# Order of VectorE and ScalarE where a transformer trunk changes over to block products on Trainium2

## The chip, the cores and the metric

The kernel runs on one core of a Trainium2 chip. The metric is the device time of one execution in microseconds; a version's time is the median of its runs. A core has TensorE (matrix products, at a clock that the chip grants it), VectorE, ScalarE, GpSimd (POOL in the profile) and SyncE (SP, which issues most transfers from memory). The engines run side by side and wait for each other on semaphores only; each takes its own instructions in their order.

## The reference, cut to what matters

The reference is a trunk of two layers over 512 tokens of width 1024 in float32. Each layer mixes tokens (two kinds of attention and a convolution, gated) and then applies a feed-forward part with 2816 hidden columns:

```python
for l in range(DEPTH):                      # 2 layers
    ...                                     # token mixing, x = x + y @ w_out[l]
    h = rmsnorm(x, norm_ffn_g[l])
    ff = jax.nn.silu(h @ w_ffn_gate[l]) * (h @ w_ffn_up[l])
    x = x + ff @ w_ffn_down[l]
```

Only the two products `h @ w_ffn_gate` and `h @ w_ffn_up` matter here.

## The kernel before, in words

**Precision.** Each float32 product is made of three passes with operands rounded for TensorE: high x high, low x high, high x low. So every weight chunk in a `raw` buffer needs a cast by ScalarE (`w_hi`, signalled on `hi_done`) and a subtraction by VectorE (`w_lo` = raw - high, signalled on `lo_done`). Four `raw` buffers form a ring that SP refills. The same is done for the activations: `h_hi` and `h_lo`.

**Two ways of making the gate and up columns.** The first six of 22 column tiles (`FRONT`) are made plainly: twelve tiles (gate, up, gate, up, ..., c = 0 to 11), 24 matmuls of 512 columns each (line 1869), each evacuated by VectorE in `front_tile` (product with `rstd_x`, L1277), with ScalarE's SiLU behind every gate tile (L1100). The other 16 are made in eight turns (`fast_turn`) of seven block products, in the manner of Strassen and Winograd: gate and up weights, and the four quadrants of the normalised activations `h_norm`, are added and subtracted in quarters so that seven products replace eight. A block product is 24 matmuls of 256 columns (L2184) and adds one to `mm_done`.

**What the first turn needs.** The four weight quarters of a turn lie in the ring: `RAW_G2`, `RAW_G1`, `RAW_U1`, `RAW_U2` (slots 0 to 3). VectorE makes the sums `first_a` = G1 + G2 and `first_b` = `first_a` + U1 (`weight_sum`, L1652, signalled on `sum_done`). ScalarE casts quarters with `cast_raw` (L1073) and sums with `cast_sum` (L1079); VectorE makes their low parts with `low` (L1649). Product 1 multiplies U1 (slot 0) by the activation quadrant `b11`; product 2 multiplies `first_a` (slot 4) by `t0`; product 3 `first_b` (slot 2) by `t1`; product 4 U2 by `b21`; product 5 takes a later sum in slot 1, product 6 one in slot 2 with `b22`, product 7 takes G2. `t0` to `t3` are differences of quadrants, made ahead. The quadrants' high parts (`half_cast`, L1067) overwrite `h_hi`, which tile 11 still reads: `b11` may be cast when tile 11's first four k steps are through (`h_free`), `b21` and `b22` when tile 11 is done. Their low parts are `half_low` (L1656).

**Order.** All orders are written out by hand. On VectorE: tile 9's work, the sum `first_a`, a wait for two casts, the sum `first_b`, the eviction of tile 10, the low parts of `first_a` and of U1, the low half of `b11`, the low part of `first_b`, the low half of `b21`, and then the turn. On ScalarE: cast of `first_a`, cast of U1, SiLU of tile 10, cast of `first_b`, `b11`, `b21`, `b22`, then G2. `LO_U1 = 1, LO_S1 = 2, LO_S2 = 3, LO_G2 = 4, LO_U2 = 5, LO_S3 = 6, LO_S4 = 7` are the places of a turn's low parts on `lo_done`; in the first turn product 1 waits for the first two. SP refills G2's slot on the fourth low part, G1's on the turn's third sum and U1's and U2's on the sixth low part. Product 7 waits for VectorE's eviction into `q5_t` (L1768), which stands behind the low part of the next turn's U1.

Of the kernel before, what the change touches and what calls it, by code (L numbers as in the profile page):

```python
# [73 lines left out]
FRONT = 6  # L74
# [78 lines left out]
RAW_G2, RAW_G1, RAW_U1, RAW_U2 = 0, 1, 2, 3  # L153
LO_G2, LO_U2, LO_S3, LO_S4, LO_U1, LO_S1, LO_S2 = 4, 5, 6, 7, 1, 2, 3
# [85 lines left out]
def trunk(nc, dram, out):  # L240
# [121 lines left out]
    first_a = at("first_a", r0 + 80 * KB, [P, 1024])  # L362
    first_b = at("first_b", r0 + 84 * KB, [P, 1024])
# [15 lines left out]
    with ExitStack() as ctx:  # L379
# [9 lines left out]
        hi_done = sem("hi_done")  # L389
        lo_done = sem("lo_done")  # L390
# [53 lines left out]
        sum_done = sem("sum_done")  # L444
# [35 lines left out]
        as_k = lambda t: t[:].rearrange("p (k c) -> p k c", k=4)  # L480
# [268 lines left out]
        def _(act):  # L749
# [168 lines left out]
            for l in layers([(ev, EVENTS), (evac, EVACS), (sqa, SQUARES), (stat, 6), (own, 1), (lr, 5), (mt, EVENTS), (olo, HEADS), (vt, PAIRS),  # L918
# [150 lines left out]
                def cast_raw(slot, which, prev):  # L1069

                    act.wait_ge(raw_ready[which], rr[which].add(16))
                    act.wait_ge(mm_done, prev)
                    nc.scalar.copy(w_hi[slot][:], raw[which][:]).then_inc(hi_done, 1)  # L1073

                def cast_sum(slot, of, n, prev):

                    act.wait_ge(sum_done, sums.value + n)
                    act.wait_ge(mm_done, prev)
                    nc.scalar.copy(as_k(w_hi[slot]), of).then_inc(hi_done, 1)  # L1079
# [9 lines left out]
                for c in range(2 * FRONT):  # L1089
                    if c < 2 * FRONT - 2:  # L1090
                        split(FF + c + 2)
                    elif c == 2 * FRONT - 2:
                        ev.add()
                        cast_raw(0, RAW_U1, ev.value)
                    if c == 0:
                        root(x_std, D, 0)
                    evac.add()
                    if c % 2 == 0:
                        act.wait_ge(evac_done, evac.value)
                        nc.scalar.activation(tmp[2][:], tmp[0][:], ACT.Silu).then_inc(sig_done, 1)  # L1100
                    for k in T_LOWS.get(c, ()):
                        act.wait_ge(half_raw, 4 * l + k + 1)
                        half_cast(t_hi[k][:], t_raw[k][:])
                    if c == 2 * FRONT - 3:
                        cast_sum(4, as_k(first_a), 1, ev.value)
                cast_sum(2, as_k(first_b), 2, ev.value)
                act.wait_ge(h_free, l + 1)
                ev.add()
                for name in HALF_ORDER:
                    if name == "b21":  # L1110
                        act.wait_ge(mm_done, ev.value)
                    if name[0] == "b":
                        r, c = int(name[1]) - 1, int(name[2]) - 1
                        half_cast(quad(h_hi, r, c), quad(h_norm, r, c))
                    elif name in LATE:
                        k = int(name[1])
                        half_cast(t_hi[k][:], t_raw[k][:])
# [95 lines left out]
        def _(dve):  # L1213
# [244 lines left out]
            for l in layers([(hi, SPLITS - 2), (mm, EVENTS), (out_n, EVACS), (own, OWN), (taps, CT * TAPS), (sig, 4 + 24 + FRONT),  # L1458
# [188 lines left out]
                def low(slot, of):  # L1647
                    dve.wait_ge(hi_done, hi.add())
                    nc.vector.tensor_tensor(as_k(w_lo[slot]), of, as_k(w_hi[slot]).bitcast(F32), ALU.subtract).then_inc(lo_done, 1)  # L1649

                def weight_sum(to, a, b):
                    nc.vector.tensor_tensor(to, a, b, ALU.add).then_inc(sum_done, 1)  # L1652
# [30 lines left out]
                for c in range(2 * FRONT - 1):  # L1683
                    if c == 0:
                        split(FF + 2)
                        factor(x_std, rstd_x)
                    front_tile(c)
                    if c == 2 * FRONT - 2:
                        dve.wait_ge(sum_done, sums.value + 2)
                        low(4, as_k(first_a))  # L1690
                        low(0, raw_k[RAW_U1])
                    elif c:
                        split(FF + c + 2)
                    if c in (H_NORM_AT, H_NORM_AT + 1):
                        for k in range(4 * (c - H_NORM_AT), 4 * (c - H_NORM_AT) + 4):
                            ins = normal(k)
                        if c > H_NORM_AT:
                            mine(ins)
                    if c == T_SUMS_AT:
                        nc.vector.tensor_tensor(t_raw[0][:], quad(h_norm, 0, 0), quad(h_norm, 0, 1), ALU.subtract).then_inc(half_raw, 1)  # L1700
                        dve.wait_ge(half_raw, 4 * l + 1)
                        nc.vector.scalar_tensor_tensor(t_raw[1][:], t_raw[0][:], -1.0, quad(h_norm, 1, 1), ALU.mult, ALU.subtract).then_inc(half_raw, 1)
                    if c == T_SUMS_AT + 1:
                        nc.vector.tensor_tensor(t_raw[2][:], quad(h_norm, 1, 1), quad(h_norm, 0, 1), ALU.subtract).then_inc(half_raw, 1)
                        dve.wait_ge(half_raw, 4 * l + 2)
                        nc.vector.scalar_tensor_tensor(t_raw[3][:], t_raw[1][:], -1.0, quad(h_norm, 1, 0), ALU.mult, ALU.subtract).then_inc(half_raw, 1)
                    for k in T_LOWS.get(c, ()):
                        half_low(t_lo[k][:], t_raw[k][:], t_hi[k][:])
                    if c == 2 * FRONT - 3:
                        first_sum(as_k(first_a))  # L1710
                        dve.wait_ge(hi_done, hi.value + 2)
                        dve.wait_ge(sum_done, sums.value + 1)
                        weight_sum(as_k(first_b), as_k(first_a), raw_k[RAW_U1])

                def half_of(name):
                    if name[0] == "t":
                        k = int(name[1])
                        half_low(t_lo[k][:], t_raw[k][:], t_hi[k][:])
                    else:
                        r, c = int(name[1]) - 1, int(name[2]) - 1  # L1720
                        half_low(quad(h_lo, r, c), quad(h_norm, r, c), quad(h_hi, r, c))

                half_of("b11")
                low(2, as_k(first_b))
                half_of("b21")

# [125 lines left out]
        def _(pe):  # L1852
# [234 lines left out]
            for l in layers([(lo, SPLITS), (part, 5 * FAST), (half, 3 * FAST), (ev, EVACS), (ea, UP_COPIES), (fl, FEEDS), (sqa, SQUARES), (std, 5), (ex, STEPS),  # L2087
# [101 lines left out]
                def fast_turn(x, start=False):  # L2189

                    y_b, q_b = bank[6], bank[7]
                    pe.wait_ge(lo_done, lo.value + (LO_S1 if start else LO_U1))
                    halves_made = HALVES_MADE * l
                    pe.wait_ge(half_lo, halves_made + HALF_AT["b11"])
                    pe.wait_ge(part_out, part.value - 5)
                    product(x, W_SLOT[0], quad(h_hi, 0, 0), quad(h_lo, 0, 0), True, False)
                    pe.wait_ge(lo_done, lo.value + LO_S1)
                    pe.wait_ge(half_out, half.value)
                    product(q_b, 4 if start else W_SLOT[1], t_hi[0], t_lo[0], True, False)
                    pe.wait_ge(lo_done, lo.value + LO_S2)  # L2200
                    pe.wait_ge(part_out, part.value + 1)
                    product(x, W_SLOT[2], t_hi[1], t_lo[1], False, False)
                    pe.wait_ge(lo_done, lo.value + LO_U2)
                    pe.wait_ge(half_lo, halves_made + HALF_AT["b21"])
                    pe.wait_ge(half_out, half.value - 2)
                    product(y_b, W_SLOT[3], quad(h_hi, 1, 0), quad(h_lo, 1, 0), True, True)
                    pe.wait_ge(lo_done, lo.value + LO_S3)
                    pe.wait_ge(half_lo, halves_made + HALF_AT["t2"])
                    pe.wait_ge(part_out, part.value + 3)
                    product(x, W_SLOT[4], t_hi[2], t_lo[2], False, False)  # L2210
                    pe.wait_ge(lo_done, lo.value + LO_S4)
                    pe.wait_ge(half_lo, halves_made + HALF_AT["b22"])
                    pe.wait_ge(part_out, part.value + 2)
                    product(q_b, W_SLOT[5], quad(h_hi, 1, 1), quad(h_lo, 1, 1), False, True)
                    pe.wait_ge(lo_done, lo.value + LO_G2)
                    pe.wait_ge(half_lo, halves_made + HALF_AT["t3"])
                    pe.wait_ge(half_out, half.value + 2)
                    product(x, W_SLOT[6], t_hi[3], t_lo[3], False, True)
                    lo.add(PRODUCTS)
                    part.add(5)  # L2220
                    half.add(3)
# [112 lines left out]
```

## Time and profile before

| | |
|---|---|
| median of 3 runs | 1709.31 us (1708.85 to 1709.51) |
| the profiled execution | 1708.57 us |
| its span | 1706.8 us |
| TensorE busy | 1686.7 us |
| VectorE busy | 1202.2 us |
| ScalarE busy | 768.3 us |
| GpSimd busy | 194.5 us |

The span is what the profile covers of one execution; 1.8 us of that execution lie around it. Ends of matmuls are modelled, so TensorE's busy share is not the share of its peak; its granted clock averages 0.997 of full speed. The change to the block products comes once in each layer, near 566 us and near 1406 us.

### The profile page before, as it was taken

Reading aid. Unit: us, or ns where it says so; the run is one execution under the profiler, and the core shown is the slowest. Engines: PE = TensorE matmul, PEld = TensorE weight load, DVE = VectorE, ACT = ScalarE, POOL = GpSimd, SP = SyncE. Lnnn points to the kernel's source line nnn. Section 1 sums busy time; section 2 is a strip of 40 time slices with the busy share of each in tenths; the row PEclk is TensorE's granted clock in tenths of the full one; section 3 lists DMA queues with packets and bytes.
Section 4 is the critical chain, followed back from the end, with each engine's and each line's share of the span. In section 5 each row is a group of like instructions: output and inputs, shape, how many; then the busy total and the mean of one; then the engine's idle time right before and its main releaser. Section 6 shows DMA issues by size and latency. Waiting matters only on the chain.

```text
span 1706.8 us, 24438 instructions
## 1 busy us (share of the span) xinstructions
PE 1686.7 (99%) x9060; PEld 1404.0 (82%) x9060; DVE 1202.2 (70%) x1699; ACT 768.3 (45%) x1236; POOL 194.5 (11%) x125
## 2 busy tenths in 40 slices
PE   9999999999999999999999999999999999999998
PEld 7777777878788899988878777778788879999887
DVE  6898887966547787763359998877755577888422
ACT  4655444343343544552245554452533434556322
POOL 0830000010020000000126210000101100000010
PEclk9999999999999999999999999999999999999999
DMA  6341221333333233333333322214333323334332
GB/s 167 81 108 50 62 55 33 110 95 95 108 99 88 74 111 103 112 97 100 93 94 71 93 62 52 55 44 111 93 92 112 98 86 100 100 98 118 90 90 74
DMA packets 277166, 152.53 MB, mean 89 GB/s; under 512 B 30356, under 2 KB 276366, under 8 KB 277068
## 3 DMA queue, kind: packets, MB, share of 16 engines
q1 hardware_dynamic: 276760, 150.96, 31.7%
q8 instruction: 63, 1.03, 0.2%
q10 hardware_dynamic: 308, 0.25, 0.1%
q14 instruction: 35, 0.29, 0.1%
HBM read 149.09 MB, written 2.10 MB: 89 GB/s over the span
## 4 chain that ended last, share of the span: by engine, by line
PE 90%; DVE 5%; ACT 2%; issue 1%; DMA 1%; POOL 1%; SPq 0%; ACTq 0%; DVEq 0%; POOLq 0%
PE bank L1869 50%; PE bank L2184 17%; PE bank L1983 12%; PE bank L2016 2%; PE bank L1995 2%; PE bank L1938 2%; PE bank L1954 1%; PE bank L2269 1%; DVE w_lo L1239 1%; DMA raw<-in_w_ffn_up 1%; PE bank L1923 1%; POOL ln_acc L640 1%; DMA raw<-in_w_in 1%; PE bank L1910 1%; ACT w_hi L1073 0%
## 5 line engine op out<-in xcount | busy, mean ns | idle before, releaser
L764 ACT CAST w_hi<-raw 128x1024 fp32r<-128x1024 f32 (+3 forms) x243 | 223.7, 921 | 464.6 <-PE bank L1869 458.0
L1239 DVE TENSOR_TENSOR w_lo<-raw,w_hi 128x1024 fp32r<-128x1024 f32 (+3 forms) x243 | 264.6, 1089 | 155.7 <-ACT w_hi L764 154.6
L1869 PE MATMUL bank<-h_hi,w_hi 128*128 128x512 f32 x672 | 267.1, 397 | 0.7 <-DVE w_lo L1239 0.4
L1869 PE MATMUL bank<-h_hi,w_lo 128*128 128x512 f32 x672 | 262.0, 390 | 0.0
L1869 PE MATMUL bank<-h_lo,w_hi 128*128 128x512 f32 x672 | 261.8, 390 | 0.0
L1316 DVE SCALAR_TENSOR_TENSOR c_acc<-u_pad,dwk_l,c_acc 128x512 f32<-128x512 f32 x240 | 189.2, 806 | 0.4
L1869 PEld LDWEIGHTS bank<-h_hi,w_hi 128*128 128x128 f32 x672 | 126.1, 188 | 35.3 <-issue 6.5
L1869 PEld LDWEIGHTS bank<-h_lo,w_hi 128*128 128x128 f32 x672 | 126.2, 188 | 26.8 <-issue 1.9
L1869 PEld LDWEIGHTS bank<-h_hi,w_lo 128*128 128x128 f32 x672 | 126.1, 188 | 26.7
L2184 PE MATMUL bank<-t_hi,w_hi 128*128 128x256 f32 x512 | 145.1, 283 | 2.4 <-DVE tmp L1768 2.3
L2184 PE MATMUL bank<-t_hi,w_lo 128*128 128x256 f32 x512 | 144.6, 282 | 0.0
L2184 PE MATMUL bank<-t_lo,w_hi 128*128 128x256 f32 x512 | 144.5, 282 | 0.0
L1983 PE MATMUL bank<-h_hi,w_hi 128*128 128x512 f32 x304 | 130.9, 431 | 0.0
L1869 PE MATMUL bank<-f_hi,w_hi 128*128 128x512 f32 x330 | 129.2, 391 | 0.0
L1869 PE MATMUL bank<-f_hi,w_lo 128*128 128x512 f32 x330 | 128.5, 389 | 0.0
L1869 PE MATMUL bank<-f_lo,w_hi 128*128 128x512 f32 x330 | 128.4, 389 | 0.0
L1983 PE MATMUL bank<-h_hi,w_lo 128*128 128x512 f32 x304 | 119.0, 392 | 0.0
L1983 PE MATMUL bank<-h_lo,w_hi 128*128 128x512 f32 x304 | 118.6, 390 | 0.0
L2184 PE MATMUL bank<-h_hi,w_hi 128*128 128x256 f32 x384 | 110.0, 286 | 6.1 <-DVE h_lo L1656 6.1
L1649 DVE TENSOR_TENSOR w_lo<-raw,w_hi 128x1024 fp32r<-128x1024 f32 x66 | 80.7, 1223 | 46.7 <-ACT w_hi L1073 46.7
L1277 DVE TENSOR_TENSOR tmp<-bank,rstd_x 128x512 f32<-128x512 f32 x76 | 52.2, 689 | 83.4 <-PE bank L1869 75.9
L2184 PE MATMUL bank<-h_hi,w_lo 128*128 128x256 f32 x384 | 109.9, 286 | 0.0
(312 smaller groups left out, 3531.2 us busy)
## 6 DMA issues: line engine op xcount, KB each, us to landing
raw<-in_w_in SPq DMA_DIRECT2D x96, 512.0 KB, 3.8
raw<-in_w_ffn_gate SPq DMA_DIRECT2D x44, 512.0 KB, 3.8
raw<-in_w_ffn_up SPq DMA_DIRECT2D x44, 512.0 KB, 4.3
raw<-in_w_ffn_down SPq DMA_DIRECT2D x32, 512.0 KB, 3.6
raw<-in_w_out SPq DMA_DIRECT2D x16, 512.0 KB, 3.7
raw<-in_w_ffn_down SPq DMA_DIRECT2D x16, 384.0 KB, 3.2
raw<-in_w_bo_a SPq DMA_DIRECT2D x16, 256.0 KB, 2.8
raw<-in_w_bo_b SPq DMA_DIRECT2D x16, 256.0 KB, 2.8
```

The source lines that it names most:

```text
L640: nc.gpsimd.tensor_tensor(acc[:], acc[:], ring[i % 2][:], ALU.add).then_inc(sq_added, 1)
L764: last = nc.scalar.copy(to, of)
L1239: last = nc.vector.tensor_tensor(to, of, part.bitcast(F32), ALU.subtract)
L1277: return nc.vector.tensor_tensor(to, s_bank[b][rows, :], by[rows, :], ALU.mult)
L1316: ins = nc.vector.scalar_tensor_tensor(c_acc[:, c, :], u_pad[:, c, k:k + T], dwk_l[:, c, k:k + 1], c_acc[:, c, :], ALU.mult, ALU.add)
L1649: nc.vector.tensor_tensor(as_k(w_lo[slot]), of, as_k(w_hi[slot]).bitcast(F32), ALU.subtract).then_inc(lo_done, 1)
L1869: ins = nc.tensor.matmul(bank_t[0:rows, :], wt[slot][:, w], x, start=first and k == 0 and p == 0, stop=last and k == k_tiles - 1 and p == 2)
L1938: nc.tensor.matmul(s_bank[score_slot(g)][:, 0:w], q_t[0:rows, head, q * P:w], k_t[0:rows, head, 0:w], start=True, stop=True).then_inc(scor ...
L1983: ins = nc.tensor.matmul(bank_t[:], wt[(QKV + n) % SPLIT][:, w], x, start=k == 0 and p == 0, stop=k == DT - 1 and p == 2, skip_group_check ...
L1995: ins = nc.tensor.transpose(t_bank[g % 2][:, k * P:(k + 1) * P], p_b[:, at_k:at_k + P], ident[:])
L2016: ins = nc.tensor.matmul(o_bank[e * VDIM:(e + 1) * VDIM, k * P:T], v_n[:, k, head * VDIM:(head + 1) * VDIM], p_t[e][:, k * (P_T_STEP + P): ...
L2184: ins = nc.tensor.matmul(bank_t[:, m * (T // 2):(m + 1) * (T // 2)], wt[:, w], x, start=first and m == 0 and k == 0 and p == 0, stop=last ...
```

## The change

On VectorE the eviction of tile 10 and the low part of U1 come ahead of the sum `first_b`, and the low part of `first_a` goes behind the low half of `b11`. On ScalarE the cast of U1 comes ahead of the cast of `first_a`, and the cast of `first_b` goes behind the cast of `b11`. TensorE's first product waits for one low part in the first turn as in the others. The waits' counts are adapted to the new order.

```diff
@@ ScalarE
                     elif c == 2 * FRONT - 2:
                         ev.add()
                         cast_raw(0, RAW_U1, ev.value)
+                        cast_sum(4, as_k(first_a), 1, ev.value)
...
-                    if c == 2 * FRONT - 3:
-                        cast_sum(4, as_k(first_a), 1, ev.value)
-                cast_sum(2, as_k(first_b), 2, ev.value)
                 act.wait_ge(h_free, l + 1)
                 ev.add()
                 for name in HALF_ORDER:
                     if name == "b21":
+                        cast_sum(2, as_k(first_b), 2, ev.value - 1)
                         act.wait_ge(mm_done, ev.value)
@@ VectorE
                     front_tile(c)
                     if c == 2 * FRONT - 2:
-                        dve.wait_ge(sum_done, sums.value + 2)
-                        low(4, as_k(first_a))
                         low(0, raw_k[RAW_U1])
+                        dve.wait_ge(sum_done, sums.value + 1)
+                        weight_sum(as_k(first_b), as_k(first_a), raw_k[RAW_U1])
...
                     if c == 2 * FRONT - 3:
                         first_sum(as_k(first_a))
-                        dve.wait_ge(hi_done, hi.value + 2)
-                        dve.wait_ge(sum_done, sums.value + 1)
-                        weight_sum(as_k(first_b), as_k(first_a), raw_k[RAW_U1])
...
                 half_of("b11")
+                dve.wait_ge(sum_done, sums.value + 2)
+                low(4, as_k(first_a))
                 low(2, as_k(first_b))
                 half_of("b21")
@@ TensorE
-                    pe.wait_ge(lo_done, lo.value + (LO_S1 if start else LO_U1))
+                    pe.wait_ge(lo_done, lo.value + LO_U1)
```

## Rows read from the trace of the kernel before

**Rows 1.** The page's first part: busy time, share of the span, instructions.

```profile
PE 1686.7 (99%) x9060; PEld 1404.0 (82%) x9060; DVE 1202.2 (70%) x1699; ACT 768.3 (45%) x1236; POOL 194.5 (11%) x125
```

**Rows 2.** TensorE's waits over the whole span, longest in total first.

```profile
engine line waited for: us in total, times, longest us
PE bank L2184 <- DVE h_lo L1656: 6.1, 2, 3.1
PE bank L2184 <- DVE tmp L1768: 2.3, 3, 1.2
```

**Rows 3.** Busy time by stretch of the first layer, with granted clock and DMA.

```profile
core 0: us, PE busy (x) PEld busy (x) DVE busy (x) ACT busy (x) POOL busy (x), PEclk, DMA share, GB/s
566.70:569.70 3.00, 0.00 (x0) 0.00 (x0) 2.69 (x4) 3.00 (x4) 0.00 (x0) 1.00 0.00 0
...
571.20:574.50 3.30, 3.30 (x18) 3.30 (x18) 1.71 (x2) 0.42 (x1) 0.00 (x0) 0.50 0.06 6
574.50:600.00 25.50, 24.56 (x204) 24.36 (x204) 20.87 (x21) 11.99 (x16) 0.00 (x0) 1.00 0.33 103
```

**Rows 4.** Timeline of TensorE: start, duration, instruction, idle before and releaser.

```profile
560.87 0.39 PE L1869 MATMUL bank<-h_hi,w_lo 128*128 128x512 f32 x1
...
563.59 0.39 PE L1869 MATMUL bank<-h_hi,w_lo 128*128 128x512 f32 x1
...
566.30 0.39 PE L1869 MATMUL bank<-h_hi,w_lo 128*128 128x512 f32 x1
569.76 0.36 PE L2184 MATMUL bank<-h_hi,w_hi 128*128 128x256 f32 x1 [3.07 <-DVE h_lo L1656]
...
573.63 0.41 PE L2184 MATMUL bank<-h_hi,w_lo 128*128 128x256 f32 x1
573.84 0.41 PE L2184 MATMUL bank<-t_hi,w_hi 128*128 128x256 f32 x1
...
579.94 0.28 PE L2184 MATMUL bank<-h_hi,w_hi 128*128 128x256 f32 x1
...
582.82 0.36 PE L2184 MATMUL bank<-t_hi,w_hi 128*128 128x256 f32 x1
...
589.74 0.36 PE L2184 MATMUL bank<-t_hi,w_hi 128*128 128x256 f32 x1 [0.94 <-DVE tmp L1768]
...
1409.89 0.36 PE L2184 MATMUL bank<-h_hi,w_hi 128*128 128x256 f32 x1 [3.07 <-DVE h_lo L1656]
```

**Rows 5.** Timeline of VectorE at the first layer's change.

```profile
560.59 1.22 DVE L1652 TENSOR_TENSOR first_a<-raw,raw 128x1024 f32<-128x1024 f32 x1
563.87 1.23 DVE L1652 TENSOR_TENSOR first_b<-first_a,raw 128x1024 f32<-128x1024 f32 x1 [2.06 <-ACT w_hi L1073]
565.01 0.68 DVE L1277 TENSOR_TENSOR tmp<-bank,rstd_x 128x512 f32<-128x512 f32 x1
565.61 1.22 DVE L1649 TENSOR_TENSOR w_lo<-first_a,w_hi 128x1024 fp32r<-128x1024 f32 x1
...
568.28 1.23 DVE L1656 TENSOR_TENSOR h_lo<-h_norm,h_hi 128x1024 fp32r<-128x1024 f32 x1 [0.31 <-ACT h_hi L1067]
...
575.64 1.22 DVE L1649 TENSOR_TENSOR w_lo<-raw,w_hi 128x1024 fp32r<-128x1024 f32 x1 [2.74 <-ACT w_hi L1073]
...
581.52 1.22 DVE L1649 TENSOR_TENSOR w_lo<-raw,w_hi 128x1024 fp32r<-128x1024 f32 x1
```

**Rows 6.** Timeline of ScalarE at the first layer's change.

```profile
561.84 1.05 ACT L1079 CAST w_hi<-first_a 128x1024 fp32r<-128x1024 f32 x1 [2.99 <-DVE first_a L1652]
562.80 1.04 ACT L1073 CAST w_hi<-raw 128x1024 fp32r<-128x1024 f32 x1
565.73 0.64 ACT L1100 ACTIVATE tmp<-tmp 128x512 f32<-128x512 f32 x1 [1.89 <-DVE tmp L1277]
...
567.21 2.94 ACT L1067 CAST h_hi<-h_norm 128x1024 fp32r<-128x1024 f32 x3
```

**Rows 7.** The chain that ended last: start, duration, what.

```profile
582.88 3.78 DMA raw<-in_w_ffn_up
...
642.26 5.04 DMA raw<-in_w_ffn_up
...
1409.89 4.62 PE bank L2184 x24
```

## The prediction, made before the changed kernel ran

> **What bounds the kernel now.** The page comes first: TensorE is busy 99% of the span [rows 1], so an edit on VectorE and ScalarE can only help where TensorE waits. The list of TensorE's waits, longest in total first, says where that is: in the whole span it waits longest for `h_lo`, twice, 6.1 us together, and next for the eviction into `q5_t` (L1768), three times, 2.3 us [rows 2]. Both lie at the change to the block products. The busy times by stretch then show what the first wait brings with it: no matmul for 3.0 us and then, 1.5 us after the restart, 3.3 us at a granted clock of 0.50, the lower level, 1.2 GHz [rows 3]. In the second layer the idle is 3.07 us too, and the first product again takes long, 4.62 us [rows 4, 7].
>
> Reading the timelines backwards from the first product (start 569.76) gives its cause. It waits for the low half of `b11`, 568.28 to 569.51 on VectorE [rows 5]. That waited for the cast of `b11`, the first of the three at 567.21 on ScalarE. In front of it ScalarE did the SiLU at 565.73, which had waited 1.89 us for the eviction of tile 10 (565.01), and the cast of `first_b` [rows 6]. The eviction stood on VectorE behind the sum `first_b` at 563.87, which had waited 2.06 us for ScalarE's cast of `RAW_U1` [rows 5], and that cast stood behind the cast of `first_a`, which waited for the sum at 560.59. Data was there long before: tile 10's last matmul starts at 560.87 and ends at 561.26, and the twelfth matmul of tile 11, after which `h_hi` may be overwritten (`h_free`), ends at 563.59 + 0.39 = 563.98 [rows 4].
>
> **The change, worked out for the first layer.** No instruction is added, removed or resized; all durations below are those of before. Back to back, VectorE starts a new 1024-column operation every 1.14 us and a new one 0.60 us after the eviction (565.01, 565.61) [rows 5]; ScalarE starts a cast every 0.95 us or so (three in 2.94 us, each 1.05 long) [rows 6].
> - *Eviction ahead of the second sum.* VectorE is free behind `first_a` at 561.73 and tile 10 is there since 561.26, so the eviction runs 561.73 to 562.42. It no longer stands behind the 2.06 us wait.
> - *`RAW_U1`'s cast first.* It needs tile 10's end only: about 561.3 to 562.4. The cast of `first_a` follows to 563.3, the SiLU to 563.9. VectorE takes the low part of `RAW_U1` at 562.4 and the sum `first_b` to about 564.8. The added wait (low part for cast) holds the sum behind it, for which only the third product's weights wait.
> - *Cast of `b11`.* ScalarE is free at 563.85, so `h_free` now decides: 564.0 to 565.1. VectorE takes its low half 565.1 to 566.35, and with the 0.25 us from its end to the first matmul seen before (569.51 to 569.76) the product starts at 566.6. Tile 11's last matmul starts at 566.30, matmuls follow each other by 0.23 us, so 566.53 is the earliest start there is. An idle of 3.07 us becomes at most 0.1.
> - *TensorE's first gate.* With `LO_U1` the first product asks for one low part, not two, so `first_a`'s, now moved behind `b11`, does not hold it.
> - *What was moved back.* Low part of `first_a`: 566.3 to 567.5, needed at 569.5 by product 2. Low part of `first_b`: cast to 566.1, low 567.4 to 568.6, needed at 572.4 by product 3. `b21`: cast from 566.7 (it waits for tile 11's end), low 568.5 to 569.7, needed at 575.3. Margins of 2.0, 3.8 and 5.6 us; without this cover each would hold TensorE one for one.
> - *DMAs.* None is issued from the moved steps. SP's loads of the next turn wait for the fourth low part or later ones and for the third sum or later, and those come earlier, not later. POOL has nothing here.
>
> **The sum.** A product at full clock ends 3.04 us after its first matmul starts (579.94 to the next one at 582.82, whose predecessor starts 0.12 before it and lasts 0.28) [rows 4]; the first after a wait takes 0.08 more (0.36 for 0.28). So product 1 ends at 566.6 + 3.12 = 569.7. Before, its last matmul began at 573.63 and ended at 574.04 [rows 4]: it now ends 4.35 us earlier. Behind it stands a chain that hangs on its end alone: copy of `r1_t`, cast and low part of `RAW_U2` (before at 575.64), two sums, eviction and product of tile 11, `b22`, low part of `RAW_U1` (581.52 to 582.74) [rows 5], then the next turn's load of `RAW_U1`, 3.78 us [rows 7], its cast, low part, and the eviction into `q5_t` that lets product 7 start at 589.74 after 0.94 us of idle [rows 4]. VectorE reaches that low part of `RAW_U2` (wanted at 571.3) with about 0.3 us in hand; past that, lateness costs one for one. Everything from there moves as a block. Product 5 becomes late next: products 1 to 4 end their issue at 578.2, its weights' low part at 578.4, so it starts near 578.5, a new wait of some 0.3 us, which costs nothing because product 7's chain still ends later, by the same 0.94 us.
>
> Second layer: product 1 starts 840.13 us after the first layer's, with the same 3.07 us of idle [rows 4], and ended at 1409.89 + 4.62 = 1414.51 [rows 7]; after, 569.7 + 840.13 = 1409.85: 4.65 us. Together 9.0 us: 6.35 of idle and 2.65 of slow matmuls. The profiled execution (1708.57, span 1706.8) becomes 1699.6 with a span of 1697.8; the median of the runs shown lies 0.7 above that execution, so 1709.3 - 9.0 = **1700.3 us**.
>
> **What the clock is worth.** The 2.65 us are in the sum because the row at 0.50 follows the only long idle, while the window with the 0.94 us idle is at 1.00 throughout [rows 3, 4]. One rule speaks against taking that for granted. The Trainium skill ("TensorE: Matmul & The Clock Gate", section "A second HAM failure mode: psum-queue depth-cycling") tells of a kernel whose short idles between groups of matmuls were frequent enough to make the clock swing between its two rates. By that rule the three short idles left in each first turn could keep some products slow; by the row they do not.
>
> **Rivals.**
> - *The slow stretch stays.* The idle goes, but a stretch like that of before still comes: 6.35 us gained, 1703.0. Against: nothing then precedes it but short idles.
> - *The load is slower.* The next turn's `RAW_U1` takes 5.04 us, as the one at 642.26 did, and not 3.78 [rows 7]; product 7 waits for it. Costs up to 1.3 us in each layer: 1702.8.
> - *No effect.* Product 1 waits for something that the profile doesn't name, and the start stays where it is: 1709.3. For it: its gate has three conditions, and the list names one of them. Against: 0.25 us from the end of `b11`'s low half to the matmul, in both layers.
> - *Slower: the clock stays down through the first turn.* Place: products 1 to 7 of each layer's first turn, kept at 0.50 by idles of 0.1, 0.3 and 0.9 us. Price: a product takes 24 x 0.21 = 5.1 us instead of 2.9 (starts 0.21 apart at 573.63 and 573.84 [rows 4]), so 2.2 us each; four such products over both layers eat the gain, six make the kernel slower by over 0.2%, and all fourteen give 1700.3 + 31 = 1731. Against: after the 0.94 us idle the clock was 1.00 [rows 3]. This is the swing which the page named above describes.
>
> **Chances and range.** Forecast 0.80, slow stretch stays 0.06, slower load 0.06, no effect 0.05, clock down 0.03. The forecast's own range is 1698.9 to 1701.5: the start of product 1 is known to 0.1 us, VectorE's 0.3 us may be used up, the waits for product 7 (0.94, and 1.2 in the second layer [rows 2]) would shrink by up to half if the load comes faster, and the three runs shown lie 0.7 apart. Taking in the two smaller gains: 1698.3 to 1703.5. Within 0.2% (3.4 us) is about what a measurement can't tell from no change: faster 0.92, same 0.05, slower 0.03.
>
> **What would show it.** In the new profile: product 1 starts 0.1 us behind tile 11, not 3.07; the stretch behind it has clock 1.00; tile 10's eviction stands directly behind `first_a`, the SiLU ends near 563.9, the cast of `b11` starts on `h_free` near 564.0; product 5 waits about 0.3 us; product 7 still waits 0.9 and 1.2 us. The prediction is wrong if the low part of `first_a` holds product 2, if `b11`'s cast starts well after 564.1, or if the granted clock falls without the idle.

## The result and the profile after

The changed kernel took 1699.33 us (median of 5 runs, 1698.98 to 1700.26) beside 1708.85 us for the kernel before (5 runs, 1707.80 to 1709.51): a ratio of 0.9945, 95% interval 0.9935 to 0.9956. That is 9.5 us less, where 9.0 were forecast; as a time, 1700.3 was forecast (range 1698.3 to 1703.5). A second set of five runs gave 1699.85 us (1699.44 to 1700.79) and 0.9952 (0.9939 to 0.9966).

The waits of TensorE over the whole span, to be read beside [rows 2]:

```profile
engine line waited for: us in total, times, longest us
PE bank L2182 <- DVE tmp L1766: 3.3, 3, 1.2
```

The wait for `h_lo` (6.1 us) has left the list; the wait of product 7 for the eviction into `q5_t` is now its first line. Line numbers have moved by one or two. TensorE's timeline at the first layer's change, for [rows 4]; the whole trace stands 0.43 us earlier here, before the change begins (`first_a` starts at 560.16 instead of 560.59):

```profile
565.87 0.39 PE L1867 MATMUL bank<-h_hi,w_lo 128*128 128x512 f32 x1
566.15 0.36 PE L2182 MATMUL bank<-h_hi,w_hi 128*128 128x256 f32 x1
...
568.98 0.28 PE L2182 MATMUL bank<-h_hi,w_lo 128*128 128x256 f32 x1
...
578.01 0.39 PE L2182 MATMUL bank<-t_hi,w_hi 128*128 128x256 f32 x1
...
585.25 0.36 PE L2182 MATMUL bank<-t_hi,w_hi 128*128 128x256 f32 x1 [1.22 <-DVE tmp L1766]
...
1402.01 0.36 PE L2182 MATMUL bank<-h_hi,w_hi 128*128 128x256 f32 x1
```

Product 1 starts 0.28 us after the start of tile 11's last matmul (565.87), with no recorded idle; in the second layer it is the same. With the 0.43 added its start is 566.58 (forecast 566.6) and its end, 568.98 + 0.28, is 569.69 (forecast 569.7). VectorE and ScalarE, for [rows 5, 6]:

```profile
560.16 1.22 DVE L1651 TENSOR_TENSOR first_a<-raw,raw 128x1024 f32<-128x1024 f32 x1
561.29 0.69 DVE L1276 TENSOR_TENSOR tmp<-bank,rstd_x 128x512 f32<-128x512 f32 x1
562.00 1.23 DVE L1648 TENSOR_TENSOR w_lo<-raw,w_hi 128x1024 fp32r<-128x1024 f32 x1
563.14 1.22 DVE L1651 TENSOR_TENSOR first_b<-first_a,raw 128x1024 f32<-128x1024 f32 x1
564.67 1.23 DVE L1655 TENSOR_TENSOR h_lo<-h_norm,h_hi 128x1024 fp32r<-128x1024 f32 x1 [0.30 <-ACT h_hi L1067]
...
570.86 1.23 DVE L1648 TENSOR_TENSOR w_lo<-raw,w_hi 128x1024 fp32r<-128x1024 f32 x1 [0.36 <-ACT w_hi L1073]
```

```profile
560.91 1.05 ACT L1073 CAST w_hi<-raw 128x1024 fp32r<-128x1024 f32 x1 [2.49 <-PE bank L1867]
561.87 1.05 ACT L1079 CAST w_hi<-first_a 128x1024 fp32r<-128x1024 f32 x1
562.82 0.63 ACT L1101 ACTIVATE tmp<-tmp 128x512 f32<-128x512 f32 x1
563.58 1.06 ACT L1067 CAST h_hi<-h_norm 128x1024 fp32r<-128x1024 f32 x1
```

The eviction stands directly behind `first_a`; the SiLU ends at 563.45, the cast of `b11` starts 0.13 us later on `h_free`, and 563.58 + 0.43 is the 564.0 of the forecast. VectorE reaches the low part of `RAW_U2` with 0.36 us in hand, so TensorE's product 1 still sets it. The stretches of [rows 3], with the second layer's:

```profile
core 0: us, PE busy (x) PEld busy (x) DVE busy (x) ACT busy (x) POOL busy (x), PEclk, DMA share, GB/s
566.15:569.65 3.50, 3.50 (x30) 3.50 (x30) 3.50 (x4) 3.30 (x4) 0.00 (x0) 1.00 0.00 0
574.50:600.00 25.50, 24.17 (x200) 23.79 (x199) 20.64 (x21) 11.47 (x14) 0.00 (x0) 1.00 0.38 112
1402.00:1406.00 4.00, 4.00 (x34) 4.00 (x34) 4.00 (x4) 3.79 (x5) 0.00 (x0) 1.00 0.01 4
```

No slow stretch is left at either change. The chain that ended last shows what now holds product 7, for [rows 7]:

```profile
566.26 3.02 PE bank L2182 x24
...
578.10 4.07 DMA raw<-in_w_ffn_up
...
583.27 0.04 DVE w_lo L1648
...
584.42 0.69 DVE tmp L1766
...
1433.38 5.80 DMA raw<-in_w_ffn_up
```

### The profile page after: what moved, and what is told of

It reads as the page before. It is cut to its first block, busy times and chain, and to the rows that moved or that the text cites. A ratio compares the mean times of both kernels' runs of the same rounds, so it can differ in the third digit from the quotient of the medians.

```text
span 1698.4 us, 24436 instructions
## 1 busy us (share of the span) xinstructions
PE 1683.3 (99%) x9060; PEld 1401.0 (82%) x9060; DVE 1202.7 (71%) x1699; ACT 768.0 (45%) x1236; POOL 194.7 (11%) x125
## 4 chain that ended last, share of the span: by engine, by line
PE 92%; DVE 4%; ACT 1%; DMA 1%; issue 1%; POOL 1%; SPq 0%; ACTq 0%; DVEq 0%; POOLq 0%
PE bank L1867 52%; PE bank L2182 16%; PE bank L1981 12%; PE bank L2014 2%; PE bank L1993 2%; PE bank L1936 2%; PE bank L1952 1%; PE bank L2267 1%; DMA raw<-in_w_ffn_up 1%; DVE w_lo L1238 1%; PE bank L1921 1%; POOL ln_acc L640 1%; DMA raw<-in_w_in 1%; PE bank L1908 1%; PE bank L1899 0%
```

## The experiments

Losses and gains below are against the changed kernel's 1699.6 us, the mean of its two medians. Only the run with the cast of U1 put back had the changed kernel beside it in the same set; the others are compared across sets, in which the kernel before had medians of 1707.9 to 1708.9, so a difference can be off by up to about 1 us.

**One part alone: the eviction.** The kernel before, with its order of casts and low parts:

```diff
                     front_tile(c)
                     if c == 2 * FRONT - 2:
+                        dve.wait_ge(hi_done, hi.value + 2)
+                        dve.wait_ge(sum_done, sums.value + 1)
+                        weight_sum(as_k(first_b), as_k(first_a), raw_k[RAW_U1])
                         dve.wait_ge(sum_done, sums.value + 2)
                         low(4, as_k(first_a))
...
                     if c == 2 * FRONT - 3:
                         first_sum(as_k(first_a))
-                        dve.wait_ge(hi_done, hi.value + 2)
-                        dve.wait_ge(sum_done, sums.value + 1)
-                        weight_sum(as_k(first_b), as_k(first_a), raw_k[RAW_U1])
```

> The kernel before, with the eviction of tile 10 alone moved ahead of the sum first_b. Theory: the eviction is one of several things in front of product 1, so this alone brings the SiLU forward to about 563.8, but the cast of first_b (sum ready at 565.1) still stands before that of b11: b11 cast 566.1, low half 567.3 to 568.5, product 1 near 568.8 instead of 569.76, an idle of 2.1 us. Gain 1.0 us a layer; whether the clock falls after an idle of 2.1 us is open: 2.0 us in all if it does, 4.7 if it does not. Rival: the eviction is the whole cause, and nearly all of the 9 us comes with it.

Measured: 1707.22 us beside 1708.80 for the kernel before, 1.6 less where 2.0 were expected; the ratio is 0.9991, and its interval (0.9981 to 1.0000) reaches no change. The profile shows an idle of 2.19 us in each layer and a granted clock of 0.50 behind both. ScalarE's timeline shows why so little came of it:

```profile
563.45 0.63 ACT L1100 ACTIVATE tmp<-tmp 128x512 f32<-128x512 f32 x1
564.83 1.05 ACT L1079 CAST w_hi<-first_b 128x1024 fp32r<-128x1024 f32 x1 [0.76 <-DVE first_b L1652]
565.79 2.93 ACT L1067 CAST h_hi<-h_norm 128x1024 fp32r<-128x1024 f32 x3
```

The SiLU is early, as wanted, but the cast of `first_b` waits for its sum and holds `b11`. The eviction alone is not the whole cause; that it is a necessary part, the run below with the eviction put back shows.

**One part withdrawn at a time.** The four others each take the changed kernel and put one step back. First the low part of `first_a`:

```diff
+                dve.wait_ge(sum_done, sums.value + 2)
+                low(4, as_k(first_a))
                 half_of("b11")
-                dve.wait_ge(sum_done, sums.value + 2)
-                low(4, as_k(first_a))
...
-                    pe.wait_ge(lo_done, lo.value + LO_U1)
+                    pe.wait_ge(lo_done, lo.value + (LO_S1 if start else LO_U1))
```

> The changed kernel, with the low part of first_a back ahead of b11's low half and product 1 waiting for two low parts. Theory: the low part runs 564.7 to 565.9, b11's low half to 567.1, product 1 starts about 0.65 us later than in the changed kernel, no fall of the clock: 1.3 us lost over both layers. Rival (the gate on one low part is what brought the gain): most of the 9 us lost.

Then the cast of `first_b`:

```diff
+                cast_sum(2, as_k(first_b), 2, ev.value)
                 act.wait_ge(h_free, l + 1)
                 ev.add()
                 for name in HALF_ORDER:
                     if name == "b21":
-                        cast_sum(2, as_k(first_b), 2, ev.value - 1)
```

> The changed kernel, with the cast of first_b back ahead of b11's. Theory: the cast waits for the sum (ready 564.4 on the changed kernel's clock), b11 follows at 565.3, product 1 comes about 1.75 us later, an idle of 1.7 us: 3.5 us lost over both layers, 6.1 if the clock falls after it. Rival: no loss, because h_free and not this cast sets b11.

Then the eviction:

```diff
-                    front_tile(c)
+                    if c < 2 * FRONT - 2:
+                        front_tile(c)
                     if c == 2 * FRONT - 2:
                         low(0, raw_k[RAW_U1])
                         dve.wait_ge(sum_done, sums.value + 1)
                         weight_sum(as_k(first_b), as_k(first_a), raw_k[RAW_U1])
+                        front_tile(c)
```

> The changed kernel, with the eviction of tile 10 back behind the sum first_b. Theory: eviction 564.3 to 565.0, SiLU to 565.6, b11 cast to 566.6, its low half to 567.8, product 1 about 1.9 us later, an idle of 1.8 us: 3.8 us lost over both layers, 6.4 if the clock falls. Rival (the eviction is the whole cause): 9 us lost.

And, together with a second set of runs of the changed kernel, the cast of U1:

```diff
-                        cast_raw(0, RAW_U1, ev.value)
                         cast_sum(4, as_k(first_a), 1, ev.value)
+                        cast_raw(0, RAW_U1, ev.value)
...
+                        dve.wait_ge(hi_done, hi.value + 2)
                         low(0, raw_k[RAW_U1])
```

> The changed kernel, with ScalarE's cast of U1 back behind that of first_a; VectorE keeps its new order and waits for both casts ahead of U1's low part. Theory: that low part starts at 563.0 on the changed kernel's clock, not 562.0, the sum first_b and behind it b11's low half move by 1.1, product 1 starts 0.8 to 1.1 us later, clock 1.00: 1.6 to 2.2 us lost over both layers. Rival: b11's cast still starts on h_free at the same time, so product 1 does too and nothing is lost.

> The changed kernel itself, unaltered, beside runs of the kernel before, as the ground for the differences in the other runs. Expected: the time that it had, 1699.3 us within 0.7, ratio 0.9945.

| put back | idle before product 1 | median us (range) | loss | expected |
|---|---|---|---|---|
| low part of `first_a` | 0.75 | 1701.54 (1701.09 to 1702.37) | 1.9 | 1.3 |
| cast of U1 | 0.93 | 1701.96 (1701.55 to 1702.15) | 2.4 | 1.6 to 2.2 |
| cast of `first_b` | 1.65 | 1703.46 (1702.70 to 1703.91) | 3.9 | 3.5, or 6.1 |
| eviction of tile 10 | 1.82 | 1705.54 (1704.57 to 1707.08) | 5.9 | 3.8, or 6.4 |

Each step put back brings a part of the idle back, and in none of the four is nothing lost or all 9 us, as the rivals have it. The first row puts back the low part of `first_a` and TensorE's gate on two low parts together; the gate was not tried by itself. The parts are not shares of a sum: the four losses add up to 14.1 us, more than the whole 9.5, because each of these steps can by itself be the last in front of `b11`'s low half. The first three rows lose 0.4 to 0.6 us more than their two idles, the last 2.3 us more (2 x 1.82 = 3.6). The stretches behind the last row's idles, first and second layer, tell where most of that comes from:

```profile
569.00:572.00 3.00, 3.00 (x27) 3.00 (x26) 3.00 (x4) 2.13 (x4) 0.00 (x0) 1.00 0.00 0
1408.00:1410.00 2.00, 2.00 (x11) 2.00 (x11) 2.00 (x2) 0.21 (x1) 0.00 (x0) 0.50 0.00 0
```

After the same 1.82 us of idle the clock stayed in the first layer and fell in the second. That gives the price of one fall, with all else equal: from the start of product 1 to the start of product 4 it is 8.71 us in the first layer (568.33 to 577.04) and 10.20 us in the second (1405.93 to 1416.13), so 1.5 us. This profiled execution, 1704.68 us, is the second lowest of the ten.

**Idle made by a wait alone.** The changed kernel with all its work in place; only product 1 of the first turn waits for something later:

```diff
-                    pe.wait_ge(lo_done, lo.value + LO_U1)
+                    pe.wait_ge(lo_done, lo.value + (LO_S2 if start else LO_U1))
```

> The changed kernel, with the first turn's product 1 waiting for first_b's low part too: an idle of about 2.2 us made by a wait alone. Theory (what is lost is the idle, plus a fixed price once the clock falls): 2.25 us a layer, 4.5 in all, if the clock stays, 7.1 if it falls. Rival (the slow stretch comes from the work behind the start, not from the idle): clock 1.00 here and in every longer idle.

and, with the low parts' wait as it was:

```diff
-                    pe.wait_ge(half_lo, halves_made + HALF_AT["b11"])
+                    pe.wait_ge(half_lo, halves_made + HALF_AT["b21" if start else "b11"])
```

> The changed kernel, with the first turn's product 1 waiting for b21's low half: an idle of about 3.3 us. Theory: 3.4 us a layer and the fall of the clock as in the kernel before (idle 3.07 us there): 6.8 + 2.65 = 9.4 us in all, the time of the kernel before. Rival (the idle is not what brings the clock down): 6.8 us and clock 1.00.

The first took 1705.85 us (1704.28 to 1706.87), 6.3 more than the changed kernel and so between the 4.5 and the 7.1 expected; the second 1710.06 us (1706.39 to 1712.27), 10.5 more and so back at the kernel before (ratio 1.0002, 0.9993 to 1.0011). The first one's idle is 2.00 us in each layer, and again one layer alone went slow, this time the first (product 1 to product 4 took 10.21 us there and 8.71 us in the second layer):

```profile
569.00:571.00 2.00, 2.00 (x11) 2.00 (x11) 1.58 (x2) 0.32 (x1) 0.00 (x0) 0.50 0.00 0
1409.00:1412.00 3.00, 3.00 (x27) 3.00 (x26) 1.94 (x2) 0.83 (x2) 0.00 (x0) 1.00 0.03 5
```

The second, with an idle of 3.29 us, fell in both. The rival, that the slow stretch comes from the work behind the start, falls: VectorE and ScalarE do the same there as in the changed kernel, which has none. The second lost 1.1 us more than the 9.4 expected. Its profile, taken of its slowest execution (1712.27 us), has the next load of U1 at 4.86 us, product 7 of the first layer idle for 2.01 us behind it, and then a third slow stretch, which the kernel before does not show in its profile (a row of TensorE's timeline, then a stretch behind it):

```profile
590.83 0.36 PE L2182 MATMUL bank<-t_hi,w_hi 128*128 128x256 f32 x1 [2.01 <-DVE tmp L1766]
592.00:594.00 2.00, 2.00 (x12) 2.00 (x11) 2.00 (x3) 0.90 (x1) 0.00 (x0) 0.50 0.00 0
```

**What is late next.** In [rows 4] and in the changed kernel, product 7 of the first turn waits for VectorE's eviction into `q5_t`. Of the products that eviction needs only product 5, but it stands behind the low part of the next turn's U1, whose load is late. So it was put ahead, in the first turn alone:

```diff
-                    else:
+                    elif not start:
                         low(0, raw_k[RAW_U1])
                     dve.wait_ge(mm_done, at_mm + 5)
                     dve.wait_ge(part_out, part.value + 2)
                     nc.vector.tensor_tensor(q5_t[:], x[:], q5_t[:], ALU.add).then_inc(half_out, 1)
+                    if start:
+                        low(0, raw_k[RAW_U1])
```

> The changed kernel, with VectorE's eviction into q5_t ahead of the low part of the next turn's U1, in the first turn alone. Theory: product 7 of the first turn waits for that low part only because the eviction stands behind it, so its idle of 1.2 and 1.1 us goes: 2.3 us faster than the changed kernel. Rival: product 7 or the next turn's product 1 waits for the late load all the same, and the time stays.

and in all turns (`if not end` in place of `if start`, and no low part ahead of it):

> As the one before, in all turns. Theory: it also removes the idle of 0.9 us that a late load (5.80 us) brought in a later turn of the changed kernel's profile: 2.3 to 3.2 us faster than the changed kernel. Rival: in the steady turns the low part of U1, now behind the eviction, comes late for the next turn's product 1 or for the sum behind it, and the time is equal or slower than with the first turn alone.

They took 1697.27 us (1696.70 to 1697.40) and 1696.20 us (1696.04 to 1696.36), 2.3 and 3.4 us less than the changed kernel; against the kernel before the second's ratio is 0.9924 (0.9910 to 0.9937). VectorE's timeline of the second, first turn:

```profile
576.93 1.22 DVE L1648 TENSOR_TENSOR w_lo<-raw,w_hi 128x1024 fp32r<-128x1024 f32 x1
...
581.38 0.69 DVE L1764 TENSOR_TENSOR tmp<-bank,tmp 128x512 f32<-128x512 f32 x1 [0.23 <-PE bank L2182]
583.36 1.22 DVE L1648 TENSOR_TENSOR w_lo<-raw,w_hi 128x1024 fp32r<-128x1024 f32 x1 [1.29 <-ACT w_hi L1073]
```

The eviction now follows product 5, and the low part still waits for the load, but nobody waits for the low part. TensorE's waits in the second kernel no longer name the eviction at all; in the first, 0.2 us are left in one later turn of each layer, behind loads of 5.09 us. Of the 1.1 us between the two, the profiles show 0.4 in these waits and 0.25 ahead of the first change, where the kernels do not differ; the rest is not accounted for. The rival, that the next turn's product 1 or the sum behind comes late instead, falls. This is the fastest version found.

## Why the prediction was right

- *Cause of the idle.* Shown: each step that the prediction named in front of `b11`'s low half brings idle back when it is put back alone (0.75 to 1.82 us), and the eviction moved alone gives 1.6 of the 9.5 us, though its interval reaches no change.
- *Start and end of product 1.* Forecast 566.6 and 569.7, measured 566.58 and 569.69 on the clock of the trace before. `h_free` decides about `b11`, as worked out.
- *The cover of what was moved back.* No product waits for `first_a`'s, `first_b`'s or `b21`'s low parts. A new wait of about 0.3 us at product 5 was foreseen: it starts at 578.01, where 566.15 and four products of 2.88 us, with 0.08 for the first, give 577.75. It starts 0.05 us behind the low part of the turn's third sum (576.74 to 577.96). In the second layer such a wait was there before the change too: product 5 started 3.18 us after product 4 (1420.07, 1423.25), not 2.88.
- *Everything behind product 1 moves as a block.* The low part of the third sum, which the prediction calls that of `RAW_U1` because it lies in that buffer, ends 4.35 us earlier on that clock (577.96 + 0.43 for 582.74). Only the load behind it did not keep its duration: 4.07 us for 3.78, so product 7 came 0.3 later than the block would have, with an idle of 1.22 us.
- *The second layer.* Product 7 after it was at 1430.42 in the trace before and is at 1421.02: 9.4 us earlier, 0.43 of them from ahead of the first change, so 9.0 as forecast. Here two small misses cancel: the first layer's product 7 gained 4.06 us and not 4.35, and tile 11 of the second layer (last matmul at 1406.43 before, 1401.73 after) shows 0.2 us more that came between the two changes and is in no term of the sum; the second layer's change gave 4.70 us for the 4.65 forecast. The spans differ by 8.4 only, mostly because of the one late load of 5.80 us at 1433.38, which cost 0.93 us in that turn. The profiled execution is the slowest of the five (1700.26). That is the "slower load" rival, which came true in single turns; the median, lower than forecast, shows no such cost, but how much of it the median carries was not measured.
- *The clock.* The slow stretch went with the idle, as forecast: clock 1.00 where it was 0.50. The 2.65 us given to it are borne out. A fall costs 1.5 us from product 1 to product 4 (start to start: 10.18 to 10.21 us in the eight profiled first turns with a fall, 8.69 to 8.71 in the sixteen without). From the start of product 1 to that of product 7, without product 7's idle, the kernel before took 19.04 and 19.37 us and the changed kernel 17.88 and 17.89, so 1.16 and 1.48, together 2.64. In the first layer part of the 1.5 us goes into the new wait of product 5. The kernel before says the same by itself: five of the 52 executions of it that were run beside the experiments have a mean granted clock of 0.999, as all of the changed kernel's have, and they took 1706.07 to 1706.85 us, 6.5 to 7.3 above the changed kernel, where 6.35 were forecast for the idle alone. The rule of the Trainium skill that spoke against it ("TensorE: Matmul & The Clock Gate", section "A second HAM failure mode: psum-queue depth-cycling") does not show here: behind idles of 0.26, 1.22 and 0.93 us the clock stayed up.
- *The 0.5 us beyond the forecast* are within what the kernel before moves by itself: its medians were 1707.9 to 1709.3 in the sets of runs.

## What to carry to other kernels

Where an engine that is in demand idles once at a change of stage, go backwards through the two or three queues in front of it and ask of each step whether the first consumer needs it; the order of the queues, not their load, was the 3 us here. Moving one step alone shows little when several stand at the same place: the steps have to be moved together, and their single effects don't add. Once the idle is gone, the next wait (here a result that stood behind an operand whose load was late) is worth the same look: it gave another 3.4 us.

## What the runs showed of the hardware that was not expected

The granted clock does not fall at one length of idle. Idles of TensorE and the clock within about 2 us behind them, from the profiled executions:

| kernel | idle us | first layer | second layer |
|---|---|---|---|
| changed, low part of `first_a` back | 0.75 | stays | stays |
| changed, cast of U1 back | 0.93 | stays | stays |
| changed, cast of `first_b` back | 1.65 | stays | stays |
| changed, eviction back | 1.82 | stays | falls |
| changed, wait for `first_b`'s low part | 2.00 | falls | stays |
| before, eviction moved alone | 2.19 | falls | falls |
| before | 3.07 | falls | falls |
| changed, wait for `b21` | 3.29 | falls | falls |

Idles of product 7, later in the same turns, belong beside them: the clock stayed behind all of 0.94 to 1.84 us and fell behind the one of 2.01 us.

In the same execution, with the same code in front, one layer kept the clock and the other lost it. The table shows one execution of each kernel; the mean granted clock of every execution, known to three digits, says how often it went so. It is 0.999 in the profiles without a fall, 0.998 in the two with one, 0.997 in the two with two and 0.996 in the one with three. Kernels with idles up to 1.65 us before product 1 have 0.999 in every execution. The kernel before, with 3.07 us twice, has 0.999 in 5 of 52 executions, 0.998 in 10, 0.997 in 24 and 0.996 in 13. So even an idle of 3 us does not seem to bring the fall each time. The spread between a kernel's lowest and highest run goes with it, though their numbers of runs differ (4 to 21): 0.3 us for the last version, 0.6 to 1.4 us for kernels with idles up to 1.65 us (the changed kernel among them), 2.5 to 2.6 us for those at 1.82 to 2.19 us, and 5.2 us (the kernel before, 1706.07 to 1711.22) and 5.9 us for the two at 3.07 and 3.29. What sets which stage is hit was not tried.
